# Value products of the sample group: three 8-column passes, or two 16-column passes with a fold

## The reference

```python
for g, (win, dil) in enumerate(((128, 1), (512, 4), (2048, 16))):
    s = einsum('bthe,btjhe->bthj', q, k[t - j * dil]) * dh ** -0.5
    p = exp(s - max(s))
    o[g] = einsum('bthj,btjhe->bthe', p, v[t - j * dil]) / sum(p)
o_b = sum(softmax(log_sum_exp)[g] * o[g] for g in range(3))
```

## Time and profile before

| | |
|---|---|
| runs | 2451.42, 2454.86, 2457.41 us |
| profiled execution | 2456.39 us; the traced span in it is 2454.7 us |
| mean granted TensorE clock | 0.977 of full |
| TensorE busy | 2294.0 us (93% of the span) |
| VectorE busy | 1608.9 us (66%) |
| ScalarE busy | 922.4 us (38%) |
| L836, matmuls | 1344, in three groups of 448 |
| L846, transposes | 64 |

### The profile page before, as it was taken

One profiled execution on the slowest core, in us unless ns is written; L12 is line 12 of the kernel. 1 busy time (PEld: TensorE's weight loads), 2 busy tenths in 40 slices (PEclk: granted clock), 3 DMA queues, 4 the chain that ended last, 5 costly groups with the idle time before them and its releaser, 6 DMA issues.

```text
span 2454.7 us, 44549 instructions
## 1 busy us (share of the span) xinstructions
PE 2294.0 (93%) x17744; PEld 2250.0 (92%) x17744; DVE 1608.9 (66%) x2085; ACT 922.4 (38%) x1326; POOL 264.8 (11%) x453
## 2 busy tenths in 40 slices
PE   5999999999999999999969999999999979999993
PEld 4999999999999999999968889888889979999993
DVE  7677877777877777777756665675666556553336
ACT  4544444444444444444423323322323333332221
POOL 0000000000000000000031221221221010000003
PEclk8999999999999999999989999999999989999996
DMA  4434433433433433443387866775774563444332
GB/s 148 121 124 124 121 114 113 125 108 119 131 104 118 121 114 113 126 134 112 112 244 201 228 220 172 231 212 157 238 220 140 168 209 114 126 135 134 104 104 91
DMA packets 400348, 358.94 MB, mean 146 GB/s; under 512 B 15664, under 2 KB 359744, under 8 KB 398368
## 3 DMA queue, kind: packets, MB, share of 16 engines
q1 hardware_dynamic: 363168, 206.28, 28.9%
q0 software_dynamic: 36992, 149.90, 19.3%
HBM read 309.74 MB, written 46.37 MB: 145 GB/s over the span
## 4 chain that ended last, share of the span: by engine, by line
PE 79%; DVE 11%; DMA 5%; issue 3%; ACT 2%; SPq 0%; POOL 0%; DVEq 0%; ACTq 0%
PE acc L699 47%; PE acc L753 25%; PE scp L836 2%; DVE prod L1436 2%; DVE far L1437 2%; DMA raw<-in_w_in 2%; DVE sc L1461 1%; PE scp L809 1%; DVE wl L1248 1%; ACT wh L959 1%; PE turn L708 1%; DMA gbuf<-gate_rows 1%; DMA cache<-in_cache_v 1%; PE turn L773 1%; DMA ones<-in_ones_k 1%
## 5 line engine op out<-in xcount | busy, mean ns | idle before, releaser
L699 PE MATMUL acc<-xh,wph 128*128 128x288 f32 x2912 | 868.6, 298 | 38.4 <-DVE wpl L1248 28.9
L699 PE MATMUL acc<-xl,wph 128*128 128x288 f32 x2912 | 860.9, 296 | 0.0
L699 PE MATMUL acc<-xh,wpl 128*128 128x288 f32 x2912 | 857.9, 295 | 0.0
L699 PEld LDWEIGHTS acc<-xh,wph 128*128 128x128 f32 x2912 | 547.6, 188 | 40.2 <-issue 23.7
L699 PEld LDWEIGHTS acc<-xh,wpl 128*128 128x128 f32 x2912 | 550.1, 189 | 0.0
L699 PEld LDWEIGHTS acc<-xl,wph 128*128 128x128 f32 x2912 | 548.7, 188 | 0.0
L1248 DVE TENSOR_TENSOR wl<-raw,wh 128x512 fp32r<-128x512 f32 x256 | 176.6, 690 | 391.1 <-ACT wh L959 390.4
L959 ACT ACTIVATE wh<-raw 128x512 fp32r<-128x512 f32 x256 | 160.8, 629 | 521.5 <-PE acc L753 473.8
L753 PE MATMUL acc<-xh,wh 128*128 128x288 f32 x1024 | 236.8, 313 | 9.6 <-DVE wl L1248 6.7
L753 PE MATMUL acc<-xl,wh 128*128 128x288 f32 x1024 | 223.6, 300 | 0.0
L753 PE MATMUL acc<-xh,wl 128*128 128x288 f32 x1024 | 223.5, 300 | 0.0
(11 more groups left out here) (212 smaller groups left out, 3616.1 us busy)
## 6 DMA issues: line engine op xcount, KB each, us to landing
raw<-in_w_in SPq DMA_DIRECT2D x128, 256.0 KB, 4.8
cache<-in_cache_v POOLq DMA_DIRECT2D x64, 448.0 KB, 5.4
w_a<-in_w_in SPq DMA_DIRECT2D x52, 512.0 KB, 3.8
w_c<-in_w_in SPq DMA_DIRECT2D x52, 512.0 KB, 3.8
w_b<-in_w_in SPq DMA_DIRECT2D x52, 512.0 KB, 3.8
w_d<-in_w_in SPq DMA_DIRECT2D x52, 512.0 KB, 4.0
ones<-in_ones_k POOLq DMA_DIRECT2D x64, 256.0 KB, 3.7
raw<-in_w_out SPq DMA_DIRECT2D x64, 256.0 KB, 2.8
```

The lines of the kernel that those rows point to most:

```text
L699: done = pe.matmul(bank, w[ring][:, k, :], a[x][:, k, :], start=(j in (0, 1, 3, 5) and k == 0 and t == 0), stop=(k == HK - 1 and t == 2), ...
```

## The change

The high and low halves of the probabilities lie side by side in one tile ps: 16 columns per sample and key tile, the high half in the first 8 and the low half in the last 8. Each value half is multiplied by all 16 in one matmul, so a key tile takes two matmuls instead of three, and the sums in PSUM have 16 rows, high rows and low rows (the product of the two low halves comes with it). When the result is turned, a matmul with the 16 x 8 matrix fold, two stacked unit matrices, adds the two sets of rows: the transposes at L846 become fp32 matmuls with 8 moving columns. osm moves from psl's place to prod's. The clearing of psl in every frame goes, and VectorE waits ahead of L1552 until the far product of step 38 has been read. ps is cleared once.

```diff
--- before.py
+++ after.py
@@ -222,15 +222,16 @@
         near = put("near", DEC_B * P)
         qb = put("qb", DEC_B, DEC_T, 32)
         qu, units = put("qu", 4, DEC_T, 32), put("units", 4, DEC_T, 32)
-        ones, prod = put("ones", 2, 4 * P), put("prod", 4, 2, P)
+        ones = put("ones", 2, 4 * P)
+        place_prod = place_v + (28 + 8 + 16 + 8 + 8 + 8) * P * 4
+        prod, osm = put("prod", 4, 2, P), sb("osm", [2 * DEC_T, 8 * P], place_prod)
         place_s = place_v + (28 + 56) * P * 4
         vh = [put("vh0", 7, P, dt=F32R), put("vh1", 7, P, dt=F32R)]
         sc = sb("sc", [P, 6 * P], place_s)
         pt = sb("pt", [P, 6 * P], place_s + CACHED * 4)
-        place_m = place_s + 2 * CACHED * 4
-        ss, psl = put("ss", KEYS + NEW), put("psl", 7 * SAMP + 4, dt=F32R)
-        osm = sb("osm", [DEC_T, 8 * P], place_m)
-        psh, mask = put("psh", 7 * SAMP + 4, dt=F32R), put("mask", 9 * P)
+        ss, ps = put("ss", KEYS + NEW), put("ps", 7 * 2 * SAMP + 16, dt=F32R)
+        mask = put("mask", 9 * P)
+        fold = sb("fold", [2 * DEC_T, DEC_T], base + 1184 - 32)
 
         m = sb("m", [P, KB, TOK], FREE)
         yb_raw = sb("yb_raw", [P, HEADS - 1, TOK], FREE)
@@ -259,10 +260,11 @@
         scp = ctx.enter_context(nc.psum_tensor("scp", [P, 1024], F32))
         accv = [acc[:, p, :].rearrange("p (h c) -> p h c", h=2)[:, :, 0:HALF] for p in range(2)]
         bank_x, bank_y, bank_w, bank_z = (accv[0][:, 0, :], accv[0][:, 1, :], accv[1][:, 0, :], accv[1][:, 1, :])
-        by_unit = lambda t: t[:, SAMP:SAMP + 136].rearrange("p (u w) -> p u w", w=68)[:, :, 0:SAMP].rearrange(
-            "p u (b x) -> p u b x", x=8)[:, :, :, 0:4]
-        by_class = lambda t: t[:, 3 * SAMP:3 * SAMP + 260].rearrange("p (c w) -> p c w", w=65)[:, :, 0:SAMP].rearrange(
-            "p c (k x) -> p c k x", x=4)[:, :, :, 0]
+        by_batch = lambda low: ps[:, 0:P].rearrange("p (b x) -> p b x", x=16)[:, :, 8 * low:8 * low + 8]
+        by_unit = lambda low: ps[:, P + 8 * low:P + 8 * low + 264].rearrange("p (u w) -> p u w", w=132)[:, :, 0:P].rearrange(
+            "p u (b x) -> p u b x", x=16)[:, :, :, 0:4]
+        by_class = lambda low: ps[:, 3 * P + 8 * low:3 * P + 8 * low + 516].rearrange("p (c w) -> p c w", w=129)[
+            :, :, 0:P].rearrange("p c (b k x) -> p c b k x", k=4, x=4)[:, :, :, 0:2, 0]
 
 
         x_in = [sem(f"x_in{i}") for i in range(5)]
@@ -284,7 +286,7 @@
         near_in, q_in = sem("near_in"), sem("q_in")
         ones_in, units_in = [sem("ones_in0"), sem("ones_in1")], sem("units_in")
         ones_sum, units_sum, far_ready = sem("ones_sum"), sem("units_sum"), sem("far_ready")
-        ps_round, ps_zero = sem("ps_round"), sem("ps_zero")
+        ps_round = sem("ps_round")
         q_spread, zeroed = sem("q_spread"), sem("zeroed")
         turned, turn_read = sem("turned"), sem("turn_read")
         scored, score_read = sem("scored"), sem("score_read")
@@ -830,11 +832,10 @@
 
                     pe.wait_ge(v_split, 8 * (f - 1) + b + 1)
                     for n in range(7):
-                        hi, lo = vh[b % 2][:, n, :], vl[:, b % 4, n, :]
-                        at = n * SAMP + DEC_T * b
-                        for t, (p, val) in enumerate(((psh, hi), (psh, lo), (psl, hi))):
-                            done = pe.matmul(scp[0:DEC_T, b * P:(b + 1) * P], p[:, at:at + DEC_T], val,
-                                             start=(n == 0 and t == 0), stop=(n == 6 and t == 2))
+                        at = 2 * (n * SAMP + DEC_T * b)
+                        for t, val in enumerate((vh[b % 2][:, n, :], vl[:, b % 4, n, :])):
+                            done = pe.matmul(scp[0:2 * DEC_T, b * P:(b + 1) * P], ps[:, at:at + 2 * DEC_T], val,
+                                             start=(n == 0 and t == 0), stop=(n == 6 and t == 1))
                     done.then_inc(pv_used, 1)
 
                 def sample_out():
@@ -843,8 +844,8 @@
                         pe.matmul(scp[:, SEQ:SEQ + SAMP], vN[par][g][0:SAMP, 4, :], psn[0:SAMP, g, :],
                                   start=(g == 0), stop=(g == GROUPS - 1))
                     for b in range(DEC_B):
-                        done = pe.transpose(scp[:, DEC_T * b:DEC_T * (b + 1)], osm[:, b * P:(b + 1) * P],
-                                            ident[0:DEC_T, 0:DEC_T])
+                        done = pe.matmul(scp[:, DEC_T * b:DEC_T * (b + 1)], osm[:, b * P:(b + 1) * P], fold[:],
+                                         start=True, stop=True)
                     done.then_inc(scored, 1)
 
                 for part in range(PARTS):
@@ -1099,10 +1100,10 @@
                                     else (pt[:, 4 * P:6 * P], turn[:, bank, 0:2 * P]))
                     elif name == ("pts", 0):
                         probs = turn[:, bank, :]
-                        copy(psh[:, 0:SAMP], probs[:, 0:SAMP]).then_inc(ps_round, 1)
-                        copy(by_class(psh), probs[:, SAMP:2 * SAMP].rearrange("p (k c) -> p c k", c=4)
+                        copy(by_batch(0), probs[:, 0:SAMP].rearrange("p (b t) -> p b t", t=8)).then_inc(ps_round, 1)
+                        copy(by_class(0), probs[:, SAMP:2 * SAMP].rearrange("p (b k c) -> p c b k", k=2, c=4)
                              ).then_inc(ps_round, 1)
-                        out = by_unit(psh)
+                        out = by_unit(0)
                         src = probs[:, 2 * SAMP:3 * SAMP].rearrange("p (b u r) -> p u b r", u=2, r=4)
                     else:
                         out, src = psn[0:SAMP], turn[0:SAMP, bank, 0:NEW].rearrange("p (n c) -> p n c", n=GROUPS)
@@ -1486,7 +1487,9 @@
                                 dve.wait_ge(consts, 48)
                                 for n_ in range(2):
                                     dve.wait_ge(v_stored[n_], 16 * (VA_PAIRS + (2 - n_) * HEADS))
-                                v.memset(psh[:].bitcast(F32), 0.0).then_inc(zeroed, 1)
+                                v.memset(ps[:].bitcast(F32), 0.0).then_inc(zeroed, 1)
+                                v.tensor_tensor(fold[:], ident[0:2 * DEC_T, 0:DEC_T], ident[0:2 * DEC_T, DEC_T:2 * DEC_T],
+                                                ALU.add).then_inc(zeroed, 1)
                             dve.wait_ge(scored, signal_no(f, "early"))
                             links.mark(masked(ss[0:SAMP, 0:P], scp[0:SAMP, 0:P], smask[0:SAMP, 0:P], small[0:SAMP, 0:1]))
                             masked(ss[0:SAMP, KEYS:], scp[0:SAMP, SEQ:SEQ + NEW], smask[0:SAMP, KEYS:],
@@ -1525,19 +1528,18 @@
                         if s == SLOT_FAR + 3:
                             dve.wait_ge(expd, 5 * f)
                             normalise(ss[0:SAMP], SAMP, 5)
-                            v.memset(psl[:].bitcast(F32), 0.0).then_inc(ps_zero, 1)
                         if s == SLOT_PTS + 1:
 
                             b0 = TURN_NAMES.index(("pts", 0)) % 2
                             dve.wait_ge(turn_read, turn_no(f, ("pts", 1)))
                             dve.wait_ge(ps_round, 2 * f)
-                            dve.wait_ge(ps_zero, f)
                             probs = turn[:, b0, :]
-                            low(psl[:, 0:SAMP], probs[:, 0:SAMP], psh[:, 0:SAMP]).then_inc(ps_split, 1)
-                            low(by_class(psl), probs[:, SAMP:2 * SAMP].rearrange("p (k c) -> p c k", c=4),
-                                by_class(psh)).then_inc(ps_split, 1)
-                            low(by_unit(psl), probs[:, 2 * SAMP:3 * SAMP].rearrange("p (b u r) -> p u b r", u=2, r=4),
-                                by_unit(psh)).then_inc(ps_split, 1)
+                            low(by_batch(1), probs[:, 0:SAMP].rearrange("p (b t) -> p b t", t=8),
+                                by_batch(0)).then_inc(ps_split, 1)
+                            low(by_class(1), probs[:, SAMP:2 * SAMP].rearrange("p (b k c) -> p c b k", k=2, c=4),
+                                by_class(0)).then_inc(ps_split, 1)
+                            low(by_unit(1), probs[:, 2 * SAMP:3 * SAMP].rearrange("p (b u r) -> p u b r", u=2, r=4),
+                                by_unit(0)).then_inc(ps_split, 1)
                         for b in range(DEC_B):
                             if s == SLOT_VS[b]:
 
@@ -1549,7 +1551,8 @@
                             spread_queries(1 - par, 64 * (f // 2 + 1))
                         if s == 39:
                             dve.wait_ge(pv_used, 8 * f)
-                            v.tensor_copy(osm[:], scp[0:DEC_T, :]).then_inc(score_read, 1)
+                            dve.wait_ge(ones_sum, 8 * f + (2 if f < HEADS else 0))
+                            v.tensor_copy(osm[:], scp[0:2 * DEC_T, :]).then_inc(score_read, 1)
                             dve.wait_ge(scored, signal_no(f, "sample_out"))
                             links.then(v.tensor_copy(otmp[:], scp[:, SEQ:SEQ + SAMP]))
                             v.tensor_tensor(otmp[:], otmp[:], scp[:, 0:SAMP], ALU.add).then_inc(score_read, 1)
```

## The result

The changed kernel took 2466.47 us in the median of 14 runs (2461.53 to 2476.48), where the kernel before, on the same chips, took 2453.07 us (14 runs, 2448.62 to 2460.32). The ratio is 1.005, 95% interval 1.0038 to 1.0062: slower by 13.4 us. I had forecast no change, with 2461 us as the upper end.

A forecast was written before the change was run, and what follows sets the result against it. TensorE, busy 93% of the span, was taken as the bound, with value landings and the osm tail also setting the pace. -13.4 + 0.8 + 10.2 + 0.7 + 3.4 = +1.7 us; forecast 2455.5 us, no change, range 2447 to 2461.

The forecast's parts named there:

- The forecast itself: Whole kernel: terms sum to +1.7 us on the profiled execution; from the median 2454.86 it forecast 2455.5, no change, chance 0.5.
- Sixteen columns: L836's stationary load, sixteen columns instead of eight: 0.8 us slower, between nothing and 1.7; 6.7 ns a load if none hidden.
- What comes through of the removed matmuls: L836's blocks, 7 of 21 matmuls removed: 13.4 us of 26.9 gained, the rest lost to waits for value splits and osm.
- The waits: TensorE's waits: for vl at blocks 4 to 6 some 1 us a frame, for osm near 1.7 us.
- The fold's own time: The turn at L846, eight transposes become fp32 matmuls of two records each: 1.28 us a frame, 10.2 us slower in all.
- The wait on ones_sum: VectorE's copy L1552 must now see L1437's end: 0.1 us in each of seven frames, 0.7 us slower.
- The clock, the step that failed: Frame boundaries: two more spells at 1.2 GHz, 1.7 us each, 3.4 us slower, from longer waits and passes.
- the rivals: Here the slower one: all seven frame boundaries fall, four more spells, 6.8 us, sum 5.1 us, 2460 us; chance 0.2.
- Costed at nothing: Copy of 16 rows, L1528's memset, finer strides, the larger memset and the fold's addition in frame 1: taken as no cost or gain.
- The strides: Finer strides of six small copies and subtractions at step 28, several parts ahead of block 0: no cost.
- the copy: Copy to osm of 16 rows for 8: no cost, as time goes by the 1024 columns a row, 1202 ns.
- the memset: L1528's clearing on VectorE at step 25, 0.435 us a frame: its removal gains nothing; 3.5 us if on the path.

The follow-up runs named there:

- e2: Changed kernel with the turn as 16-row transposes and the halves added by VectorE, instead of the fold matmuls: 2444.96 us, ratio 0.9964 to the kernel before.
- e7: e2 with VectorE's far product of step 34 moved to step 29, ahead of block 0: 2443.89 us, ratio 0.9948 to the kernel before.
- e1: Kernel before with only the turn changed, eight transposes of osm made fp32 matmuls with the 8 x 8 unit matrix: 2474.11 us, ratio 1.0087.
- e9: Kernel before with one extra VectorE copy (448 columns of osm) ahead of L1552, lengthening TensorE's wait for osm: 2465.27 us, ratio 1.0035.
- e3: Changed kernel with ten unused matmuls a frame filling TensorE's wait for osm: 2457.36 us, ratio 1.0011 to the kernel before.
- e10: Changed kernel, fold included, with TensorE's part of step 39 moved behind the frame's last gate part: 2455.73 us, ratio 0.9997 to the kernel before.
- e4: Kernel before with ten unused matmuls a frame ahead of TensorE's wait for osm: 2454.89 us, ratio 1.0003.

## Why the prediction was wrong

*The forecast itself.* 2454.86 + 1.7 is 2456.6 and not the 2455.5 that I wrote; the range does not hang on it.

*Sixteen columns.* The matmul took 60 ns, as at the lower end. The 0.8 us that I added were not there. The load's own record grew from 89 to 95 ns, twice the 3 ns that I had taken, but the step from matmul to matmul stayed at 60 ns. Nor did the 6.7 ns show in the step that I had estimated from the Trainium skill's figure for a load (TensorE: Matmul & The Clock Gate, section LDWEIGHTS): the record's 6 ns are near it, and they are hidden here.

*What comes through of the removed matmuls.* Forecast 13.4 us, measured 13.4 us in sum up to L844. By frames it was 1.2, 2.5, 1.7, 1.9, 1.1, 2.0, 1.0 and 2.0 us where I had said 1.0, 1.1, 1.7, 1.1, 1.7, 1.7, 1.7 and 3.4: the landing of the moment decides it. The sum came out by errors that cancel, and by luck: in e2's trace, with the same two passes, it is 9.5 us. Frame 8 fell short most: blocks 6 and 7 waited for their splits there too. The mechanism, load, rounding, two splits and the far product between them, stands by block 5 in the trace and by e7.

*The waits.* For vl I had some 1 us a frame; it was 6.5 us in sum. For osm I had near 1.7 us; it was up to 1.9.

*The fold's own time.* 1.28 us a frame forecast, 1.88 - 0.59 = 1.29 measured where the clock stayed up. Right. The nearest row was L843's.

*The wait on ones_sum.* 0.1 us forecast, 2.54 - 2.35 = 0.19 us measured, 0.6 us more over seven frames.

*The clock, the step that failed.* I had "two boundaries more, 3.4 us", at 1.7 us each. It was four boundaries more, all seven, and the price was wrong by more than the count: most stretches at 1.2 GHz last 6.8 us or more and not 3.4, and in five frames they cover part of the turn, which then costs 2.4 to 3.5 us and not 1.9. In the two traces that is up to 20.4 us, over all runs some 14, and not 3.4. The mechanism was among the rivals, with the right place and side, but its price, four stretches of 1.7 us and 5.1 us in sum, was taken from the short stretches of the kernel before. e1 and e9 show that wait and fold each bring all seven boundaries down. e3 and e10 show that with less of the idle wait 9 and 11 us come back with the fold still there (in e10, 6 of the 11 are the wait itself), and the clock over all runs shows that the fold is the larger part.

*Costed at nothing.* The strides (228 ns for a subtraction into ps, 227 before) and the copy (1212 for 1202 ns) were worth nothing, as said. No experiment takes out the memset alone.

## What to carry to other kernels

A change that saves work on TensorE ahead of a wait for another engine makes that wait longer; cost not the wait alone but also what the clock does behind it, above all where small passes follow, and take that cost from an experiment if the trace has only short falls. One trace is one execution: the granted clock of all runs says how typical it is. Turn stacked halves with transposes and add them on the engine that reads PSUM anyway, rather than with fp32 matmuls that load 128 columns twice to move eight. Where an engine waits at a fixed place of an order written by hand, look first whether one more piece of its own work can go ahead of the wait.

## What I had not expected of the hardware

0.65 us more of idleness a frame (e9, 2.0 us at most instead of 1.3) took the boundaries at the lower clock from three to seven, and cost two to two and a half times its own length in all, the idleness included. Unused matmuls in the wait gave back 9 us where the fold followed (e3) and nothing where transposes followed (e4). In the frames the stretches at the lower clock were 3.4, 6.8 or 10.2 us long. At seven of the fourteen boundaries of e9 and the change the lower clock set in 0.2 to 1.0 us after the end of the wait, while TensorE was already at work again; before, 1.4 to 1.6 us after it.
